# Attention scores from split query and key halves stacked on 128 rows, with a reordered first and last stage

## The reference, cut to what matters

```python
proj = einsum('bsd,dn->bsn', rms_norm(x, g_pre), w_in)
qa, ka, va, fa, za, qb, kb, vb, zb, gates = split(proj)
# fox attention: 8 heads of width 64, causal
logits = qa @ ka.T / sqrt(64) + c[t] - c[s]      # c: running sum of log-forget gates
ya = softmax(mask(logits)) @ va * silu(za)
# differential attention: 4 heads, two maps (q1,k1) and (q2,k2) of width 64 each, causal
qd, kd = apply_rope(qb), apply_rope(kb)
yb = (softmax(q1 @ k1.T / 8) - lam * softmax(q2 @ k2.T / 8)) @ vb
yb = rms_norm(yb, g_subln) * (1 - lam_init) * silu(zb)
merged = sigmoid(gate_a) * (ya @ w_branch[0]) + sigmoid(gate_b) * (yb @ w_branch[1])
x = x + rms_norm(merged @ w_out, g_post)
```

## Time and profile before

| | |
|---|---|
| median of 3 executions | 2862.41 us (2861.88 to 2864.34) |
| profiled execution | 2862.21 us, of which its span 2860.4 us |
| busy share of the span | PE 90%, PEld 73%, DVE 35%, ACT 25%, POOL 25% |
| matmuls | 12814 |
| mean granted clock of TensorE | 0.945 of full speed |
| DMA | 170.09 MB, mean 59 GB/s |

### The profile page before, as it was taken

One profiled execution on the slowest core, in us unless ns is written; L12 is line 12 of the kernel. 1 busy time (PEld: TensorE's weight loads), 2 busy tenths in 40 slices (PEclk: granted clock), 3 DMA queues, 4 the chain that ended last, 5 costly groups with the idle time before them and its releaser, 6 DMA issues. The chain is left out here.

```text
span 2860.4 us, 32356 instructions
## 1 busy us (share of the span) xinstructions
PE 2580.4 (90%) x12814; PEld 2080.7 (73%) x12814; DVE 1001.0 (35%) x1466; ACT 714.4 (25%) x1041; POOL 708.6 (25%) x437
## 2 busy tenths in 40 slices
PE   5899997599739899999999989799999989996987
PEld 4677776589728688888888868677777766674876
DVE  4055534444343521312213350133332314555423
ACT  3134454022211210201102121244442014443012
POOL 2111113133323232433334313111111221110221
PEclk9999998699959899999999989899999999998998
DMA  5411111222221111111111113112112111112422
GB/s 161 89 34 37 38 38 55 52 54 67 67 85 52 37 45 51 44 51 45 50 51 44 51 30 103 53 41 63 57 52 92 39 30 45 45 45 78 143 69 94
DMA packets 230734, 170.09 MB, mean 59 GB/s; under 512 B 40209, under 2 KB 213047, under 8 KB 229856
## 3 DMA queue, kind: packets, MB, share of 16 engines
q1 hardware_dynamic: 217888, 135.01, 16.8%
q10 hardware_dynamic: 12736, 33.56, 3.3%
HBM read 129.67 MB, written 38.88 MB: 59 GB/s over the span
## 5 line engine op out<-in xcount | busy, mean ns | idle before, releaser
L253 POOL CAST Wh<-Wraw 128x1024 fp32r<-128x1024 f32 x155 | 163.0, 1052 | 1757.9 <-PE PS L282 744.3
L255 POOL TENSOR_TENSOR Wl<-Wraw,Wh 128x1024 fp32r<-128x1024 f32 x155 | 399.5, 2577 | 22.4
L282 PE MATMUL PS<-XAh,Wh 128*128 128x512 f32 x520 | 165.7, 400 | 8.3 <-POOL Wl L255 4.2
L282 PE MATMUL PS<-XAl,Wh 128*128 128x512 f32 x520 | 161.7, 392 | 0.0
L282 PE MATMUL PS<-XAh,Wl 128*128 128x512 f32 x520 | 161.4, 392 | 0.0
L282 PE MATMUL PS<-XBl,Wh 128*128 128x512 f32 x520 | 160.1, 389 | 0.0
L282 PE MATMUL PS<-XBh,Wh 128*128 128x512 f32 x520 | 160.1, 389 | 0.0
L282 PE MATMUL PS<-XBh,Wl 128*128 128x512 f32 x520 | 160.0, 389 | 0.0
L282 PE MATMUL PS<-Fh,Wl 128*128 128x512 f32 x512 | 157.6, 389 | 0.0
L282 PE MATMUL PS<-Fh,Wh 128*128 128x512 f32 x512 | 157.6, 389 | 0.0
L282 PE MATMUL PS<-Fl,Wh 128*128 128x512 f32 x512 | 157.6, 389 | 0.0
(11 more groups left out here) (374 smaller groups left out, 5019.6 us busy)
## 6 DMA issues: line engine op xcount, KB each, us to landing
Wraw<-in_w_in SPq DMA_DIRECT2D x67, 512.0 KB, 4.0
Wraw<-in_w_ffn_in SPq DMA_DIRECT2D x32, 512.0 KB, 4.0
Wraw<-in_w_ffn_out SPq DMA_DIRECT2D x32, 512.0 KB, 3.9
x_scr<-hT SPq DMA_DIRECT2D x2, 4096.0 KB, 12.9
Wraw<-in_w_out SPq DMA_DIRECT2D x16, 512.0 KB, 4.7
gate_scr<-gbuf ACTq DMA_DIRECT2D x16, 512.0 KB, 2.6
gin<-gate_scr ACTq DMA_DIRECT2D x8, 1024.0 KB, 7.4
xtok<-in_x SPq DMA_DIRECT2D x4, 1024.0 KB, 8.4
```

Source lines behind the costliest of these rows:

```text
L253: pool.tensor_copy(Wh[:, slot], Wraw[:, slot])
L255: pool.tensor_tensor(Wl[:, slot], Wraw[:, slot], Wh[:, slot].bitcast(F32), ALU.subtract).then_inc(w_ready, 1)
L282: mm = pe.matmul(PS[:, 2 * slot + b, :], w[:, slot, k], x[:, b * 512:(b + 1) * 512], start=(c == 0 and m == 0), stop=(c == len(xs) - 1 and ...
```

## The change

1. Scores of both attentions. `st_h` and `st_l` (or `rt_h`, `rt_l` behind the rotation) take the hi and lo part of a query or key tile; both go to DRAM (`qs_scr`, `ks_scr`). Per head (or map) six DMAs of 64 rows of 4 KB bring back three tiles of 128 rows: `q` with hi on the upper 64 rows and lo on the lower, `kh` with the key's hi part twice, `kl` with its lo part twice. `map_scores` then does two `float32r` matmuls for each piece, `q` by `kh` and `q` by `kl`, and the same mask matmul. There are buffers for two heads.
2. ACT and DVE both work on each of the eight tiles of `phase9`, and `ps_free` comes from DVE. DVE's final scaling of `hT` is spread over the first four tiles.
3. SP loads the first two heads in `phase10` and in `phase13`, later heads in between the weight tiles of `phase11` and `phase14`, each behind a wait on the scores of the head before the last. `Ya` goes to DRAM in `phase12` and comes back in `phase15`.
4. First stage: the transposes of tokens go ahead of that of `vecs`; POOL splits the first two weight tiles in `phase0`, not in `phase1`.
5. Last stage: `turned(j - 1)` stands in the middle of product `j`; ACT's and DVE's token copies go ahead of the next scaling; DVE finishes all eight row blocks, the last in two halves, and ACT and POOL none.

```diff
 def pe_phase0(pe):
-    pe.wait_ge(vec_in, N_VEC)
-    pe.transpose(PS[:, 7, 0:V_ROWS], vecs[:], ...).then_inc(pv_psum, 1)
     for g in range(2 * KT):
...
+    pe.wait_ge(vec_in, N_VEC)
+    pe.transpose(PS[:, 4, 0:V_ROWS], vecs[:], ...).then_inc(pv_psum, 1)
...
+def pool_phase0(pool):
+    for j in range(2):
+        split_q(pool, j)
...
+def store_halves(eng, j, hi, lo, out_sem):
+    scr = qs_scr if j < 4 else ks_scr
+    eng.dma_start(scr[0, j % 4], hi.bitcast(F32)).then_inc(out_sem, 16)
+    eng.dma_start(scr[1, j % 4], lo.bitcast(F32)).then_inc(out_sem, 16)
+def load_map(eng, g, bufs, in_sem):
+    half = slice(HD * (g % 2), HD * (g % 2) + HD)
+    q, kh, kl = bufs
+    for dst, scr, top, bottom in ((q, qs_scr, 0, 1), (kh, ks_scr, 0, 0), (kl, ks_scr, 1, 1)):
+        eng.dma_start(dst[0:HD].bitcast(F32), scr[top, g // 2, half]).then_inc(in_sem, 16)
+        eng.dma_start(dst[HD:P].bitcast(F32), scr[bottom, g // 2, half]).then_inc(in_sem, 16)
+def map_scores(pe, bufs, i, dst):
+    q, kh, kl = bufs
+    for c, w in pieces(i):
+        for x in (kh, kl):
+            mm = pe.matmul(dst(c)[:, 0:w * P], q[:, i * P:(i + 1) * P], x[:, c * 512:c * 512 + w * P],
+                           start=(x is kh), stop=(x is kl and c != i // 4))
+    return pe.matmul(dst(c)[:, (w - 1) * P:w * P], identb[:], diagb[:], start=False, stop=True)
...
 def dve_phase9(dve):
...
     dve.wait_ge(ms_done, 4)
+    for j in range(8):
+        dve.wait_ge(qk_hi, j + 1)
+        dve.scalar_tensor_tensor(st_l[:, j % 2], pair(...), ..., st_h[:, j % 2], MULT, SUBTRACT).then_inc(qk_lo, 1)
+        dve.wait_ge(qk_lo, j + 1)
+        dve.sem_inc(ps_free, 1)
+        # two of the eight hT products
...
 def sp_phase10(sp):
+    for i in range(2):
+        sp.wait_ge(qk_out[i], 128)
     sp.dma_start(diagf[:], ...)
+    for h in range(2):
+        load_map(sp, h, fox_bufs[h], qk_in[h])
...
 def sp_phase11(sp):
-    load_range(sp, N_ZA + 2, N_QB + 2)
+    for _, what, x in sorted(todo):
+        if what == "tile":
+            load_range(sp, x, x + 1)
+        else:
+            sp.wait_ge(f_s, NT * (x - 1))
+            load_map(sp, x, fox_bufs[x % 2], qk_in[x % 2])
...
 def scores(u):
+    if i == 0:
+        pe.wait_ge(qk_in[h % 2], 96 * (h // 2 + 1))
-    mm = pe.matmul(PS[...], Qa[r, h // 2, i * P:(i + 1) * P], Ka[r, h // 2, ...], start=True, stop=not last)
+    map_scores(pe, fox_bufs[h % 2], i, lambda c: PS[:, 2 + 2 * (u % 2) + c]).then_inc(f_s, 1)
...
 def pe_phase18(pe):
-        product(pe, N_OUT2 + j, (N_OUT2 + j) % 2, merged)
-        if j:
-            turned(j - 1)
+        product(pe, N_OUT2 + j, (N_OUT2 + j) % 2, merged, lambda k: turned(j - 1) if j and k == 4 else None)
```

More of the change, by code:

```diff
@@ L542, in pool_phase1 @@
             pool.memset(cpad[0][:, S + 2:S + 4], 0.0)
[L543 to L550, removed]
+            for j in range(2, 4):
+                split_q(pool, j)
             pool.wait_ge(spill, 16)
@@ L1669, in sp_phase11 @@
         def sp_phase11(sp):
-            load_range(sp, N_ZA + 2, N_QB + 2)
+            todo = [((i - 1) * FOX_STEPS / len(FOX_FILL), "tile", N_ZA + 2 + i) for i in range(len(FOX_FILL))]
+            todo += [(FOX_STEPS * (h - 1) / H8, "head", h) for h in range(2, H8)]
+            for _, what, x in sorted(todo):
[4 more added lines that the diff above has]
+                    load_map(sp, x, fox_bufs[x % 2], qk_in[x % 2])
         def pool_phase11(pool):
@@ L1869, in act_phase12 @@
                 act.activation(VbT[:, j], pair(n % 2), ACT.Copy).then_inc(ps_free, 1)
+            act.wait_ge(ya_out, 16)
+            for i in range(2):
+                act.wait_ge(rq_out[i], 128)
         def dve_phase12(dve):
@@ L1892, in sp_phase13 @@
                 sp.dma_start(lrow[:, i], a[name].partition_broadcast(P)).then_inc(lam_in, 16)
+            for h in range(2):
+                load_head(sp, h)
             sp.wait_ge(lam_in, 64)
@@ L1927, in sp_phase14 @@
         def sp_phase14(sp):
-            load_range(sp, N_ZB + 2, N_BR + 2)
+            todo = [((i - 1) * DIFF_STEPS / len(DIFF_FILL), "tile", N_ZB + 2 + i) for i in range(len(DIFF_FILL))]
+            todo += [(DIFF_STEPS * (h - 1) / GH, "head", h) for h in range(2, GH)]
+            for _, what, x in sorted(todo):
+                if what == "tile":
+                    load_range(sp, x, x + 1)
+                else:
+                    sp.wait_ge(b_s, 2 * NT * (x - 1))
+                    load_head(sp, x)
         def pool_phase14(pool):
@@ L1941, in scores @@
                 h, i = divmod(u, NT)
+                if i == 0:
+                    pe.wait_ge(rq_in[h % 2], 192 * (h // 2 + 1))
                 for m in range(2):
-                    r = slice(HD * m, HD * m + HD)
                     if u >= 1:
                         pe.wait_ge(b_exp, 2 * (u - 1) + m + 1)
[L1946 to L1950, removed]
+                    map_scores(pe, diff_bufs[h % 2][m], i, lambda c: PS[:, 2 + 2 * m + c]).then_inc(b_s, 1)
             def turn(u, c, w):
@@ L2261, in dve_phase18 @@
                 if j:
+                    tokens(j - 1)
                     dve.drain()
```

126 lines of the change are left out of this document (80 added, 46 removed).

## The result

The changed kernel takes 2769.91 us (2768.72 to 2777.31, four executions) against 2862.14 of the kernel before on the same chip: a ratio of 0.968 (0.9665 to 0.9701). The forecast was 2781 with a range of 2765 to 2808. The profiled execution took 2770.20 us, span 2768.4, so 92.0 less than before, where the working came to 81.8.

The account below looks back on a forecast made before the run. PE's own instruction stream was taken to bound both attention stages. Scores -68.6, projection stage +0.7, first stages -10.7 and last stage -3.2 sum to -81.8 us from 2862.21: 2781 us, range 2765 to 2808.

Parts of the forecast that it names:

- PE's stream bounds both attentions; the pace is that of the products.: Both attention stages last as long as PE's instructions; new float32r score matmuls start 0.228 us apart at 512 columns.
- B: Each of a head's 24 new score matmuls shows about 0.109 us of weight load: 2823 us; chance 4%.
- C: Narrow float32r score matmuls run at float32 pace, 6.7 us less gain: 2788 us; chance 11%.
- A: PE waits for softmax in every attention unit of one to four blocks, 21.6 us of gain lost: 2802; chance 7%.
- a group's cost was counted from its first score: Scores of both attentions: from first score to mask, 9.37 us a head falls to 5.08, saving 68.6 us in all.
- So nothing moves: `phase10`: SP's twelve more DMA issues ahead of `cum`, 5.2 us at 0.43 each, delay it by nothing.
- nothing again: `phase13`: 24 issues behind the lambda rows take 10.3 us and end before the stage does; 0, bound 2 us.
- the signs of being right: Among them: PE's waits under 5 us in both attentions, no wait on a map's DMA, fox stage about 302 us.
- Projection stage, +0.7: PE's next product waits for DVE's first subtraction until about 1707.85: 0.7 us longer, once.
- First stages, -10.7: Earlier token transposes give 6.2 us, no wait for POOL's splits in `phase1` 4.5: 10.7 us saved, bounds 8.5 and 11.5.
- Last stage, -3.2: Column sums end 1.5 us earlier, DVE's row blocks take 1.7 less: 3.2 us saved, bounds 2.5 and 3.7.
- `phase12`, 0: The chain from a rotation to its low half grows to some 7 us in a period of 12.7: no change.

Follow-up runs that it names:

- the repeat: The changed kernel run again, unaltered, as the reference of a later group: 2767.56 us, ratio 0.967 to the kernel before.

## Why the prediction was right, and where it was not

- **PE's stream bounds both attentions; the pace is that of the products.** Right: 4.99 us a head for 5.08, no wait at a turning behind the first or at a differential combination. Rivals B and C are wrong: matmuls at 512 columns start 0.23 apart, and a group of one block, both matmuls and all, takes 0.26 us where C wanted over 0.4. A is wrong too, since no unit behind the first waited for softmax. The 0.109 us for a matmul of 128 columns, read as the pace of the weight load, was too dear: two of them start 0.060 apart in the second piece of a group.
- **The step that failed: a group's cost was counted from its first score.** The entry of 0.2 us lies ahead of that, and no term of the sum had it. With the entries the term would have been 69.3 + 16.7 = 86.0, for the 85.9 measured (81.7 and the 4.2 of the longer first wait).
- **"So nothing moves" at `cum`, and "nothing again" in `phase13`.** Both wrong, by some 4 us and 4.6 us. The issues were counted at 0.43 us for 0.60. `cum` was issued 11.2 us behind the stage's start, just as before; it landed late, since ACT could issue the loads of the gates only at 1841.07. The transfers were counted at the rate of a 128-row one in the earlier trace rows: 3 MB take some 13 us at 240 GB/s and start only behind the lambda rows. The bounds of 3 and 2 us were too narrow, and `cum`'s place behind 3 MB on one queue was not priced at all. Three of the signs of being right failed: PE's waits in the two stages came to 12.8 us where under 5 were allowed, there was a wait on a map's DMA, and the fox stage took 306.6 us for 302. The 302 was misread besides: it takes 34 from a window of 336.0 us that ends 10.9 us before the stage does.
- **Projection stage, +0.7:** right; PE's product waits 1.4 us for DVE where it had waited 0.77 for POOL. **First stages, -10.7:** 7.8 in the first trace, 9.8 in the repeat and 10.3 for those edits alone. **Last stage, -3.2:** 4.2 in the changed kernel and 3.5 for the edits alone. Its rows are as forecast, nine of DVE's in 9.8 us where the earlier trace rows has six in 11.43:

```profile
2754.75 9.78 DVE L2358 SCALAR_TENSOR_TENSOR ytok<-ytok,rpost,htok 128x1024 f32<-128x1024 f32 x9
```

- **`phase12`, 0:** it got 2.9 us shorter, by the clock and by no edit of mine to price. PE at the start of that stage, before, after, and after again (column before the last two: granted clock):

```profile
2190.90:2197.00 6.10, 6.09 (x23) 5.52 (x24) 0.00 (x0) 0.00 (x0) 0.00 (x0) 0.51 0.82 279
```

```profile
2143.90:2150.00 6.10, 6.10 (x35) 5.36 (x36) 0.00 (x0) 0.00 (x0) 0.00 (x0) 1.00 0.80 279
```

```profile
2139.00:2145.10 6.10, 6.06 (x28) 5.53 (x29) 0.00 (x0) 0.00 (x0) 0.00 (x0) 0.72 0.78 280
```

So some 16 us of gain at the entries, 3 of clock and 1 in the last stage stand against 9 us of late loads and 3 of the first stages, two of which vary from run to run: the time came out 11 us below the forecast, inside the range. The mechanism was right, but that it came so near owes something to luck: errors of 20 and 12 us stood against each other.

## What to carry to other kernels

Count a group of instructions from the instruction in front of it to the one behind it; a change of the number of rows between matmuls costs about 0.1 us each way here, and 64-row matmuls scattered among 128-row ones pay it twice. Check the shape of a DMA as well as its bytes: 128 plain rows moved at 415 GB/s, two halves of 64 rows at 244, and 2 x 64 rows in one DMA at 53. Where a small transfer that gates a stage stands in a queue, put large ones that are due later behind it.

## What the runs showed of the hardware

- A 64-row matmul among 128-row ones: 0.09 to 0.17 us more on entry, 0.09 on exit, and 0.02 to 0.075 between the first two of a group, for float32 and for float32r; 31 to 33 us of this kernel.
- Two float32r matmuls of 128 columns start 0.060 us apart inside a group, in proportion to the 0.23 at 512. At a group's start they don't: the pair of a one-block group and the way to its mask take 0.26 us (0.14 and 0.12).
- Loads of 64 rows fill the 16 DMA engines at 244 GB/s, of 128 rows at 415. With a DRAM source whose outer dimension is 2 the share is that of 2 engines (0.13, 53 GB/s), and from the third load on SP stands 9.8 us in each issue.
- After PE's idle 2.1 us ahead of `phase12` the granted clock was 0.51, 0.72 or 1.00 over the next 6 us; the stage then took 155, 154 or 152 us. The three kernels with float32 scores (before, its ends alone, float32 on 128 rows) showed 155, all with float32r scores and the stores of the change 152 or 154. What decides it is open.
